# A fused transformer forward pass on one core: order of work in attention block one's last six steps, and the split of the convolution's last group between engines

## The chip, the core and the metric

The kernel runs on one core of a Trainium2 chip. The metric is the device time of one execution in microseconds (us). Before the change the median of three runs is 1892.98 us (1890.98 to 1897.77). Every time below is from one profiled execution of that kernel, which took 1893.7 us and whose first to last instruction span 1891.7 us; "at 237.29" means 237.29 us after the span's start.

## What is computed

Two transformer blocks run over 512 tokens of width 1024 (batch 1). The parts that matter here are the attention of block one and the convolution of block two's odd layer:

```python
# block one: differential attention, 8 heads of 2 x 64, in query blocks of 128
s1 = einsum('bhqd,bkhd->bhqk', qa, k1) + bias      # bias = -slope * |pq - pos|
s2 = einsum('bhqd,bkhd->bhqk', qb, k2) + bias
a = softmax(s1) - lam * softmax(s2)
o = einsum('bhqk,bkhd->bqhd', a, v)
o = rmsnorm(o, subln_g) * (1.0 - lam_init)         # over a head's 128
x = x + g1 * (o.reshape(B, S, H * dv) @ w_out)
# block two, odd layer: gated projection, depthwise convolution of 31 taps, layer norm, projection
h = h[..., :CONV_DIM] * sigmoid(h[..., CONV_DIM:])
y = causal_dwconv(h, dw_w, dw_b)                   # width 31, 1024 channels
y = silu(layer_norm(y, ln_g, ln_b)) @ w_pw2
```

Between and after them stand a mixture of 16 experts, a second attention with pooling, and two gated feed-forward layers with a convolution of width 3.

## The kernel before

Everything is kept transposed, channels on the 128 partitions and the 512 tokens along the row; `x` is eight such chunks (KC = 8). Each weight chunk of 128 x 1024 floats is split by ScalarE into a rounded part (`split_hi`, line 118) and by VectorE into the rest (`split_lo`, line 123), and `product` (lines 950 to 960) multiplies with three matmuls: high by high, low activation by high weight, low weight by high activation. The order on each engine is written by hand; the engines meet through semaphores, and each engine's queue is strictly in order. PSUM is the one tensor `ps`, 8 banks of 128 x 512 floats.

**Attention of block one.** A step g (0 to 31) is one head (g // 4) and one query block of 128 (g % 4). On TensorE a step has `scores` (line 1019, two 128 x 512 results, into banks 0 and 1 for even g, 2 and 3 for odd g), `turn` (line 1029, four transposes of the combined probabilities into bank 4) and `values` (line 1040, four matmuls). VectorE has `biased` (line 1652, adds the distance bias and takes the row maximum; line 1658 negates it), `combined` (lines 1666, 1668 and 1671, softmax one minus lambda times softmax two), and `copy_o` (line 1677). ScalarE has `exps` (line 567, two halves), `evict_turned` (line 575) and `squares_of_o` (line 583). While the loop runs over g, TensorE makes scores two steps ahead; VectorE does `combined(g + 1)`, then `biased(g + 2)`, then `copy_o(g)`. In steps 0 to 25 TensorE fills the rest of each step with half a projection of queries or keys (`qk_part`). From step CARRY = 26 on there is no such projection left; TensorE turns a finished head's output back (`turn_o(g - 26)`, line 1051), ScalarE and VectorE make its two parts (`o_hi`, line 593; `o_lo`, line 1692). After the loop come `turn_o(5)` and `turn_o(6)`, then the output projection: `two_products` makes output chunks 0 and 1 together, input chunk by input chunk (k = 0 to 7, six matmuls each, with `turn_o(7)` ahead of k = 4), and the chunks m = 2 to 7 follow one at a time in banks 4 and 5, each after `x_new` of chunk m - 2. VectorE adds each to `x` (line 1737) and in between works through columns of the conditioning matrix (`late_column`, line 1602).

**Convolution.** Channel chunks are called groups q = 0 to 7. Of a group's 31 taps, ScalarE with GpSimd makes 9 (products at line 894, sums at line 2292), TensorE 6 (`taps`, line 1524, a matmul with a diagonal matrix that ScalarE has built, line 885) and VectorE 16 (`taps_dve`, lines 2142 and 2148), accumulating in PSUM; lines 2152 and 2154 add the parts. Group 7 stands behind the loop. Then the layer norm: TensorE sums the channels with a matmul by ones (`rms_sum`, line 923), VectorE scales the mean (line 1563), TensorE spreads it over partitions (`spread`, line 929), VectorE subtracts it from all eight chunks (line 2180), ScalarE squares them (line 477), and TensorE sums the squares, this time after `wait_ge(centred, KC)`, all eight subtractions. `unread` (line 935) issues matmuls whose results nobody reads: one ahead of chunk 7's sum, two behind it, four behind the spread, in both passes.

## Time and profile before

| | |
|---|---|
| median of 3 runs | 1892.98 us |
| the profiled execution, and its span | 1893.7 us, 1891.7 us |
| TensorE matmuls busy | 1815.9 us |
| VectorE, ScalarE, GpSimd busy | 1188.0, 907.8, 184.3 us |
| mean granted TensorE clock | 0.972 |
| attention's last steps and first two output chunks | about 225 to 266 us |
| the convolution's group 7 and its layer norm | about 1425 to 1467 us |

### The profile page before, as it was taken

Reading aid. Unit: us, or ns where it says so; the run is one execution under the profiler, and the core shown is the slowest. Engines: PE = TensorE matmul, PEld = TensorE weight load, DVE = VectorE, ACT = ScalarE, POOL = GpSimd, SP = SyncE. Lnnn points to the kernel's source line nnn. Section 1 sums busy time; section 2 is a strip of 40 time slices with the busy share of each in tenths; the row PEclk is TensorE's granted clock in tenths of the full one; section 3 lists DMA queues with packets and bytes.
Section 4 is the critical chain, followed back from the end, with each engine's and each line's share of the span. In section 5 each row is a group of like instructions: output and inputs, shape, how many; then the busy total and the mean of one; then the engine's idle time right before and its main releaser. Section 6 shows DMA issues by size and latency. Waiting matters only on the chain.

```text
span 1891.7 us, 26051 instructions
## 1 busy us (share of the span) xinstructions
PE 1815.9 (96%) x8494; PEld 1408.8 (74%) x8494; DVE 1188.0 (63%) x1838; ACT 907.8 (48%) x1379; POOL 184.3 (10%) x219
## 2 busy tenths in 40 slices
PE   7999989899999789999999999999996999999999
PEld 5777677688888567667788888886663778888887
DVE  6777775788898572454566665224997566656422
ACT  3566641488788534554444434115663544444310
POOL 0000000222322100001000000001763000000000
PEclk8999988699999989999999999999997999999999
DMA  9533141899999451111233233331210222332331
GB/s 401 178 101 98 48 135 66 316 347 374 381 376 367 172 182 49 45 41 34 78 102 98 89 103 109 99 89 45 67 67 23 78 78 89 100 100 89 112 99 56
DMA packets 72785, 259.20 MB, mean 137 GB/s; under 512 B 10256, under 2 KB 10384, under 8 KB 71440
## 3 DMA queue, kind: packets, MB, share of 16 engines
q1 hardware_dynamic: 67536, 247.85, 37.7%
q0 software_dynamic: 4608, 8.40, 1.2%
q10 hardware_dynamic: 576, 2.10, 0.3%
q8 instruction: 40, 0.66, 0.1%
q14 instruction: 25, 0.20, 0.0%
HBM read 254.11 MB, written 12.58 MB: 141 GB/s over the span
## 4 chain that ended last, share of the span: by engine, by line
PE 89%; DVE 4%; issue 2%; ACT 2%; DMA 1%; SPq 0%; DVEq 0%; POOL 0%; ACTq 0%; POOLq 0%
PE ps L958 19%; PE ps L960 19%; PE ps L959 19%; PE ps L1140 3%; PE ps L1141 3%; PE ps L1142 3%; PE ps L935 2%; PE ps L1524 2%; PE ps L1160 1%; PE ps L1162 1%; PE ps L1161 1%; PE ps L1019 1%; PE ps L1040 1%; PE ps L978 1%; PE ps L979 1%
## 5 line engine op out<-in xcount | busy, mean ns | idle before, releaser
L958 PE MATMUL ps<-h_hi,w_hi 128*128 128x512 f32 x1184 | 473.9, 400 | 0.7 <-DVE x L1737 0.5
L960 PE MATMUL ps<-h_hi,w_lo 128*128 128x512 f32 x1184 | 462.3, 390 | 0.0
L959 PE MATMUL ps<-h_lo,w_hi 128*128 128x512 f32 x1184 | 461.7, 390 | 0.0
L123 DVE TENSOR_TENSOR w_lo<-raw,w_hi 128x1024 fp32r<-128x1024 f32 x212 | 266.4, 1260 | 190.1 <-ACT w_hi L118 184.9
L118 ACT ACTIVATE w_hi<-raw 128x1024 fp32r<-128x1024 f32 x212 | 221.5, 1049 | 205.4 <-PE ps L960 168.6
L958 PEld LDWEIGHTS ps<-h_hi,w_hi 128*128 128x128 f32 x1184 | 222.7, 188 | 75.6 <-issue 31.8
L960 PEld LDWEIGHTS ps<-h_hi,w_lo 128*128 128x128 f32 x1184 | 222.6, 188 | 47.4
L959 PEld LDWEIGHTS ps<-h_lo,w_hi 128*128 128x128 f32 x1184 | 222.9, 188 | 46.9 <-issue 2.9
L2091 DVE SCALAR_TENSOR_TENSOR tmp<-ps,param,tmp 128x511 f32<-128x511 f32 (+1 forms) x176 | 131.8, 749 | 133.4 <-ACT tmp L846 121.4
L162 DVE TENSOR_TENSOR w_lo<-ring,w_hi 128x1024 fp32r<-128x1024 f32 x128 | 149.9, 1220 | 30.6 <-ACT w_hi L158 30.5
L846 ACT ACTIVATE tmp<-ps,param 128x512 f32<-128x512 f32 x88 | 68.5, 779 | 179.5 <-PE ps L960 179.5
L958 PE MATMUL ps<-gv_hi,w_hi 128*128 (+1 forms) x352 | 139.1, 395 | 0.0
L960 PE MATMUL ps<-gv_hi,w_lo 128*128 (+1 forms) x352 | 139.0, 395 | 0.0
L959 PE MATMUL ps<-gv_lo,w_hi 128*128 (+1 forms) x352 | 139.0, 395 | 0.0
L158 ACT ACTIVATE w_hi<-ring 128x1024 fp32r<-128x1024 f32 x128 | 128.7, 1055 | 12.3 <-PE ps L1142 12.3
L2202 POOL TENSOR_TENSOR pool_carrier<-const 128x1 f32<-128x1 f32 x74 | 33.9, 459 | 678.1 <-DVE x L2115 432.8
L2292 POOL TENSOR_TENSOR part<-prod,part 128x512 f32<-128x512 f32 x64 | 84.8, 1326 | 55.4 <-ACT prod L894 51.0
L1140 PE MATMUL ps<-w_hi,e_hi 128*128 128x512 f32 x192 | 78.9, 411 | 5.6 <-DVE e_lo L1828 5.6
L960 PEld LDWEIGHTS ps<-gv_hi,w_lo 128*128 128x128 f32 x352 | 66.0, 187 | 16.2
L162 DVE TENSOR_TENSOR m_lo<-ring,m_hi 128x1024 fp32r<-128x1024 f32 x64 | 76.6, 1219 | 2.3 <-ACT m_hi L158 2.3
L959 PEld LDWEIGHTS ps<-gv_lo,w_hi 128*128 128x128 f32 x352 | 66.0, 187 | 16.2
L958 PEld LDWEIGHTS ps<-gv_hi,w_hi 128*128 128x128 f32 x352 | 66.0, 187 | 16.1
(310 smaller groups left out, 2782.1 us busy)
## 6 DMA issues: line engine op xcount, KB each, us to landing
ring<-in_w_m SPq DMA_DIRECT2D x192, 512.0 KB, 5.8
raw<-in_w_b SPq DMA_DIRECT2D x180, 512.0 KB, 3.5
raw<-in_w_a SPq DMA_DIRECT2D x32, 512.0 KB, 4.0
ada_late<-in_ada_b SPq DMA_DIRECT2D x32, 512.0 KB, 4.4
ada<-in_ada_a SPq DMA_DIRECT2D x8, 1024.0 KB, 17.0
y_tok<-y_dram SPq DMA_DIRECT2D x8, 512.0 KB, 6.9
x<-in_x SPq DMA_DIRECT2D x2, 1024.0 KB
h_dram<-h_tok ACTq DMA_DIRECT2D x4, 512.0 KB, 3.5
```

The costliest lines, as they stand in the source:

```text
L118: act.activation(self.hi[:, s, :], self.raw[:, s, :], ACT.Copy).then_inc(self.hi_done, 1)
L123: dve.tensor_tensor(self.lo[:, s, :], self.raw[:, s, :], self.hi[:, s, :].bitcast(F32), ALU.subtract).then_inc(self.lo_done, 1)
L158: act.activation(self.hi[c % PARTS_M], self.ring[:, c % RING], ACT.Copy).then_inc(self.hi_done, 1)
L162: dve.tensor_tensor(self.lo[c % PARTS_M], self.ring[:, c % RING], self.hi[c % PARTS_M].bitcast(F32), ALU.subtract).then_inc(self.lo_done, 1)
L846: act.activation(tmp[:, c], ps[:, c], ACT.Identity, scale=PR_at("ffn_w", it, 6, 3 * p + (f * 2 + val) * 3 * FC + 2), bias=PR_at("ffn_b", i ...
L958: pe.matmul(dst, hi, a_hi, start=first, stop=False, skip_group_check=True)
L959: pe.matmul(dst, hi, a_lo, start=False, stop=False, skip_group_check=True)
L960: return pe.matmul(dst, lo, a_hi, start=False, stop=last, skip_group_check=True)
L1140: pe.matmul(ps[:, bank], e_hi[:, k], hi, start=(k == 0), stop=False, skip_group_check=True)
L1141: pe.matmul(ps[:, bank], e_lo[:, k], hi, start=False, stop=False, skip_group_check=True)
L2091: dve.scalar_tensor_tensor(out=tmp[:, c, back:], in0=ps[:, c, 0:T - back], scalar=PR_at("ffn_w", it, 6, 3 * p + (f * 2 + val) * 3 * FC + tap),
L2292: pool.tensor_tensor(part[:, p], prod[:, n % 4], part[:, p], ALU.add).then_inc(part_step, 1)
```

## The change

It has two parts. **In attention**, from step 26 on, all scores go to banks 0 and 1 (`s_bank`) and each waits for `biased` of the step before; TensorE makes scores three steps ahead instead of two (in step 26 both `scores(28)` and `scores(29)`); VectorE does `biased(g + 2)` ahead of `combined(g + 1)`; banks 2 and 3, now free, hold output chunks 0 and 1, whose share of input chunk k is issued by `first_outputs(k)`, k = 0 to 3 inside steps 28 to 31, k = 4 behind `turn_o(6)`, then `turn_o(7)` (now in bank 7) and k = 5 to 7. Output chunks 2 and 3 no longer wait for an addition to `x`; chunk m from 4 on waits for chunk m - 2 as before.

**In the convolution**, group 7 gets 16 taps on TensorE and 6 on VectorE (`last_taps`). The ten additional diagonal matrices lie in the first half of `act_out` and are made by ScalarE ahead of the convolution's loop. VectorE accumulates its six taps in banks 6 and 0, adds them up, adds GpSimd's part, and last TensorE's. In the mean's pass the `unread` matmuls ahead of and behind chunk 7's sum are gone (the four behind the spread stay), and TensorE no longer waits for all eight subtractions ahead of the sums of squares; each sum waits for its own square.

TensorE, last steps of attention. Here `hd_qk` rows are `scores`, `const,tmp` rows `turn`, `v,at_pt` rows `values`, `const,o` rows `turn_o`, and `h_hi,w_hi` to `h_hi,w_lo` a `product`. Before, from `scores(28)` on:

```order
L1019 MATMUL ps<-hd_qk 128x512 x2
L1029 MATMUL ps<-const,tmp 128x128 x4
L1040 MATMUL ps<-v,at_pt 128x128 x4
L1051 MATMUL ps<-const,o 128x128 x4
L1019 MATMUL ps<-hd_qk 128x512 x2
L1029 MATMUL ps<-const,tmp 128x128 x4
L1040 MATMUL ps<-v,at_pt 128x128 x4
L1051 MATMUL ps<-const,o 128x128 x4
L1019 MATMUL ps<-hd_qk 128x512 x2
```

After, from `scores(28)` on:

```order
L1031 MATMUL ps<-hd_qk 128x512 x2
L1041 MATMUL ps<-const,tmp 128x128 x4
L1052 MATMUL ps<-v,at_pt 128x128 x4
L1063 MATMUL ps<-const,o 128x128 x4
L1031 MATMUL ps<-hd_qk 128x512 x4
L1041 MATMUL ps<-const,tmp 128x128 x4
L1052 MATMUL ps<-v,at_pt 128x128 x4
L1063 MATMUL ps<-const,o 128x128 x4
L1031 MATMUL ps<-hd_qk 128x512 x2
L1041 MATMUL ps<-const,tmp 128x128 x4
L1052 MATMUL ps<-v,at_pt 128x128 x4
L1063 MATMUL ps<-const,o 128x128 x4
```

`scores(29)` and `scores(30)` now stand together behind `turn_o(0)`, the latter a step earlier than before; behind the last row shown come six matmuls of `first_outputs(0)`.

VectorE in step 26. `hd_bias` rows are `biased`, the rows with `at_r`, `at_c` and `tmp<-tmp,at_c` are `combined`, `o<-o,o_r` is `scale_o(4)` and `o<-ps,at_r` is `copy_o(26)`. Before:

```order
L1666 RECIPROCAL at_r<-at_sum 128x2
L1668 TENSOR_SCALAR at_c<-at_r,at_sum,neg_lam 128x1
L1671 SCALAR_TENSOR_TENSOR tmp<-tmp,at_c 128x512
L1650 MEMSET carrier 128x1
L1652 ISA tmp,at_m<-ps,hd_bias 128x512
L1652 ISA at_m 128x1
L1652 ISA tmp,at_m<-ps,hd_bias 128x512
L1652 ISA at_m 128x1
L1658 TENSOR_SCALAR at_nm<-at_m 128x2
L1688 TENSOR_TENSOR o<-o,o_r 128x4x128
L1677 TENSOR_SCALAR o<-ps,at_r 128x128
```

After:

```order
L1681 MEMSET carrier 128x1
L1683 ISA tmp,at_m<-ps,hd_bias 128x512
L1683 ISA at_m 128x1
L1683 ISA tmp,at_m<-ps,hd_bias 128x512
L1683 ISA at_m 128x1
L1689 TENSOR_SCALAR at_nm<-at_m 128x2
L1697 RECIPROCAL at_r<-at_sum 128x2
L1699 TENSOR_SCALAR at_c<-at_r,at_sum,neg_lam 128x1
L1702 SCALAR_TENSOR_TENSOR tmp<-tmp,at_c 128x512
L1719 TENSOR_TENSOR o<-o,o_r 128x4x128
L1708 TENSOR_SCALAR o<-ps,at_r 128x128
```

`biased(28)` moved ahead of `combined(27)`, and so in each of steps 26 to 29.

TensorE behind the convolution's loop, before (`glu,diag` is `taps`, `conv,ones` and `tmp,ones` are the sums, `ps<-const` is `unread`, `junk,const` is `spread`):

```order
L1524 MATMUL ps<-glu,diag 128x512 x6
L923 MATMUL ps<-conv,ones 32x128 x28
L935 MATMUL ps<-const 128x512
L923 MATMUL ps<-conv,ones 32x128 x4
L935 MATMUL ps<-const 128x512 x2
L929 MATMUL ps<-junk,const 128x128 x4
L935 MATMUL ps<-const 128x512 x4
L923 MATMUL ps<-tmp,ones 32x128 x28
```

After:

```order
L1556 MATMUL ps<-glu,diag 128x512 x6
L1556 MATMUL ps<-glu,act_out 128x512 x10
L934 MATMUL ps<-conv,ones 32x128 x32
L940 MATMUL ps<-junk,const 128x128 x4
L946 MATMUL ps<-const 128x512 x4
L934 MATMUL ps<-tmp,ones 32x128 x28
```

Ten matmuls with a diagonal came in ahead of the sums, and three `unread` matmuls went.

The diff, without the declarations of banks and semaphores that the words above give:

```diff
         def o_bank(h):
-            return SSQ if h < 5 else h - 5
+            return SSQ if h < 5 or h == H - 1 else h - 5
+        def s_bank(g):
+            return 0 if g >= CARRY else g % 2 * 2
+        def p_bank(m):
+            return 2 + m if m < 2 else 4 + m % 2
...
         STEPS = NT * H
...
+            for j in range(LAST_MORE):
+                act.activation(diag_last[:, j], C("ident"), ACT.Copy,
+                               scale=PR("dw_w", (KC - 1) * TAPS + POOL_TAPS + PE_TAPS + j, 1)).then_inc(diag_more, 1)
             conv_act(0, True)
...
                 conv_act(it, False)
...
                 for k in range(first, KC):
-                    if k == KC - 1:
+                    if k == KC - 1 and n != MEAN:
                         unread(1)
                     rms_sum(n, k, src)
-                unread(2)
+                if n != MEAN:
+                    unread(2)
                 pe.wait_ge(rstd_done, n + 1)
...
                 unread(4)
...
                 if g >= 2:
-                    pe.wait_ge(s_free, g - 1)
+                    pe.wait_ge(s_free, g if g > CARRY else g - 1)
                 for half in range(2):
                     d = slice(half * DH, (half + 1) * DH)
-                    last = pe.matmul(ps[:, g % 2 * 2 + half], hd_qk[d, h % 2, 0, q * P:(q + 1) * P], hd_qk[d, h % 2, 1, :],
+                    last = pe.matmul(ps[:, s_bank(g) + half], hd_qk[d, h % 2, 0, q * P:(q + 1) * P], hd_qk[d, h % 2, 1, :],
                                      start=True, stop=True, skip_group_check=True)
...
                     pe.wait_ge(acc_free, 2 * H)
-                elif h < 5:
-                    pe.wait_ge(hlo_done, KC + h)
+                elif h < 5 or h == H - 1:
+                    pe.wait_ge(hlo_done, KC + min(h, 5))
                 pe.wait_ge(o_scaled, h + 1)
...
                 last.then_inc(o_tr, 1)
+            def first_outputs(k):
+                parts_made(k, KC)
+                for m in range(2):
+                    if k == 0:
+                        sa.ready(pe, 6, m)
+                    last = product(ps[:, p_bank(m)], sa.parts(m, k), k, k == 0, k == KC - 1)
+                    if k == KC - 1:
+                        last.then_inc(sa.used, 1)
...
             for half in range(2):
...
             for g in range(STEPS):
-                if g + 2 < STEPS:
+                if g <= CARRY:
                     scores(g + 2)
+                elif g + 3 < STEPS:
+                    scores(g + 3)
                 if g < CARRY:
...
                 if g + 1 < STEPS:
...
                     turn_o(g - CARRY)
-            def last_heads(k):
-                if k == 4:
-                    turn_o(H - 1)
+                if g == CARRY:
+                    scores(g + 3)
+                if g >= CARRY + 2:
+                    first_outputs(g - CARRY - 2)
...
             turn_o(H - 2)
+            first_outputs(4)
+            turn_o(H - 1)
+            for k in range(5, KC):
+                first_outputs(k)
             pe.wait_ge(o_copied, STEPS - 1)
-            two_products(6, 0, 4, lambda k: KC, sa, last_heads)
             for m in range(2, KC):
                 sa.ready(pe, 6, m)
-                pe.wait_ge(x_new, m - 1)
+                if m >= 4:
+                    pe.wait_ge(x_new, m - 1)
                 for k in range(KC):
-                    last = product(ps[:, 4 + m % 2], sa.parts(m, k), k, k == 0, k == KC - 1)
+                    last = product(ps[:, p_bank(m)], sa.parts(m, k), k, k == 0, k == KC - 1)
                 last.then_inc(sa.used, 1)
...
                 pe.wait_ge(sq_done, q + (MEAN * KC - 1))
-                for j in range(PE_TAPS):
-                    last = pe.matmul(ps[:, 4 + p], diag[:, p, j], glu[:, p, POOL_TAPS + j:POOL_TAPS + j + T],
-                                     start=(j == 0), stop=(j == PE_TAPS - 1), skip_group_check=True)
+                more = LAST_MORE if isinstance(q, int) and q == KC - 1 else 0
+                if more:
+                    pe.wait_ge(diag_more, more)
+                for j in range(PE_TAPS + more):
+                    by = diag[:, p, j] if j < PE_TAPS else diag_last[:, j - PE_TAPS]
+                    last = pe.matmul(ps[:, 4 + p], by, glu[:, p, POOL_TAPS + j:POOL_TAPS + j + T],
+                                     start=(j == 0), stop=(j == PE_TAPS + more - 1), skip_group_check=True)
                 last.then_inc(pe_taps, 1)
             def chunk_pair(it, first):
...
             rms_sums(MEAN, src=conv, first=KC - 2)
-            pe.wait_ge(centred, KC)
             rms_sums(7)
...
             ffn_pe(1, 8, 6 * KC + NG, 28, 2)
...
                     last = dve.tensor_tensor_reduce(
-                        out=at_p[:, g % 2 * 2 + half], in0=ps[:, g % 2 * 2 + half],
+                        out=at_p[:, g % 2 * 2 + half], in0=ps[:, s_bank(g) + half],
                         in1=hd_bias[:, h % 2, (NT - 1 - q) * P:(NT - 1 - q) * P + T], scale=1.0, scalar=-BIG,
...
                 last.then_inc(s_free, 1)
...
             for g in range(STEPS):
+                if g >= CARRY and g + 2 < STEPS:
+                    biased(g + 2)
                 if g + 1 < STEPS:
...
                     o_lo(g - CARRY - 1)
-                if g + 2 < STEPS:
+                if g < CARRY:
                     biased(g + 2)
...
                     sa.split_lo(dve, 0, KC + 3 + g // 2 + AHEAD)
...
                 sa.multiplied(dve, 6, m)
-                dve.scalar_tensor_tensor(out=x[:, m], in0=ps[:, 4 + m % 2], scalar=mod[:, 2 * KC + m:2 * KC + m + 1],
+                dve.scalar_tensor_tensor(out=x[:, m], in0=ps[:, p_bank(m)], scalar=mod[:, 2 * KC + m:2 * KC + m + 1],
                                          in1=x[:, m], op0=ALU.mult, op1=ALU.add).then_inc(x_new, 1)
...
+            def last_taps():
+                q, p, own, fresh = KC - 1, 1, ps[:, 5], (ps[:, RB], ps[:, 0])
+                count = DVE_TAPS - LAST_MORE
+                for n in range(count):
+                    j = TAPS - count + n
+                    src, w, acc = glu[:, p, j:j + T], PR("dw_w", q * TAPS + j, 1), fresh[n % 2]
+                    if n >= 2:
+                        dve.wait_ge(dve_tap, q * DVE_TAPS + (n - 1))
+                        ins = dve.scalar_tensor_tensor(out=conv[:, q] if n == count - 2 else acc, in0=src, scalar=w, in1=acc,
+                                                       op0=ALU.mult, op1=ALU.add)
+                    elif n:
+                        ins = dve.tensor_scalar(acc, src, w, None, ALU.mult)
+                    else:
+                        ins = dve.tensor_scalar(acc, src, w, PR("dw_b", q, 1), ALU.mult, ALU.add)
+                    ins.then_inc(dve_tap, 1)
+                dve.wait_ge(dve_tap, q * DVE_TAPS + count)
+                dve.tensor_tensor(conv[:, q], conv[:, q], fresh[1], ALU.add).then_inc(dve_tap, 1)
+                dve.wait_ge(part_done, q + 3)
+                dve.wait_ge(dve_tap, q * DVE_TAPS + count + 1)
+                dve.tensor_tensor(conv[:, q], conv[:, q], part[:, p], ALU.add).then_inc(merged, 1)
+                dve.wait_ge(pe_taps, q + 3)
+                dve.wait_ge(merged, q + 1)
+                dve.tensor_tensor(conv[:, q], conv[:, q], own, ALU.add).then_inc(sq_done, 1)
             def conv_pair(it, first):
                 for c in range(SLOTS):
...
                 conv_pair(it, False)
-            taps_dve(KC // 2 - 1, 1)
+            last_taps()
             rms_spread(MEAN, mean=True)
...
             for k in range(KC):
```

## Rows read from the trace of the kernel before

**Rows 1.** Page, part 1: busy time, share of the span, instructions.

```profile
PE 1815.9 (96%) x8494; PEld 1408.8 (74%) x8494; DVE 1188.0 (63%) x1838; ACT 907.8 (48%) x1379; POOL 184.3 (10%) x219
```

**Rows 2.** Timeline, TensorE, 226 to 255: start, us, engine, line, names, [idle before <- releaser].

```profile
226.94 0.66 PE L1029 MATMUL ps<-const,tmp 128*128 128x128 f32 x4 [0.75 <-DVE tmp L1671]
...
228.85 1.13 PE L1019 MATMUL ps<-hd_qk 64*128 64x512 f32 x4
...
237.29 0.66 PE L1029 MATMUL ps<-const,tmp 128*128 128x128 f32 x4 [2.57 <-DVE tmp L1671]
237.78 1.06 PE L1040 MATMUL ps<-v,at_pt 128*128 128x128 f32 x8
...
248.46 1.11 PE L1029 MATMUL ps<-const,tmp 128*128 128x128 f32 x4 [2.73 <-DVE tmp L1671]
```

**Rows 3.** Timelines of VectorE and ScalarE, one step of attention (237.99 to 243.38).

```profile
237.99 0.69 DVE L1652 CUSTOM_DVE_ANT_0 tmp<-ps,hd_bias 128x512 f32<-128x512 f32 x1
...
241.08 0.17 DVE L1666 RECIPROCAL at_r<-at_sum 128x2 f32<-128x2 f32 x1 [1.33 <-ACT tmp L567]
...
243.38 0.75 DVE L1692 SCALAR_TENSOR_TENSOR h_lo<-ps,subln,h_hi 128x512 fp32r<-128x512 f32 x1 [1.03 <-ACT h_hi L593]
...
239.53 0.72 ACT L567 ACTIVATE tmp<-tmp,at_nm 128x512 f32<-128x512 f32 x1 [2.25 <-DVE at_nm L1658]
```

**Rows 4.** Timelines around the output projection's third chunk: TensorE, then VectorE.

```profile
266.45 0.47 PE L958 MATMUL ps<-h_hi,w_hi 128*128 128x512 f32 x1 [0.47 <-DVE x L1737]
...
272.08 0.43 PE L923 MATMUL ps<-tmp,ones 128*32 128x128 f32 x8
...
274.64 0.74 DVE L1737 SCALAR_TENSOR_TENSOR x<-ps,mod,x 128x512 f32<-128x512 f32 x1
```

**Rows 5.** Windows of 1 us: busy time of each engine, granted clock (PEclk), DMA.

```profile
1427.00:1428.00 1.00, 1.00 (x3) 0.48 (x2) 1.00 (x2) 1.00 (x3) 0.12 (x1) 0.82 0.89 295
...
1431.00:1432.00 1.00, 1.00 (x4) 0.52 (x3) 1.00 (x2) 0.37 (x2) 0.92 (x2) 0.97 0.00 0
```

**Rows 6.** Timeline, VectorE, the convolution's group 7 and the mean.

```profile
1437.53 0.81 DVE L2142 TENSOR_SCALAR ps<-glu,param 128x512 f32<-128x512 f32 x1
1438.24 8.64 DVE L2148 SCALAR_TENSOR_TENSOR ps<-glu,param,ps 128x512 f32<-128x512 f32 x13
...
1448.31 0.70 DVE L2152 TENSOR_TENSOR ps<-ps,part 128x512 f32<-128x512 f32 x1
1449.04 0.69 DVE L2154 TENSOR_TENSOR conv<-conv,ps 128x512 f32<-128x512 f32 x1
1450.50 0.29 DVE L1563 TENSOR_SCALAR junk<-ps 128x128 f32<-128x128 f32 x1 [0.78 <-PE ps L923]
1455.52 4.87 DVE L2180 TENSOR_TENSOR conv<-conv,ps 128x512 f32<-128x512 f32 x8 [4.72 <-PE ps L929]
```

**Rows 7.** Timeline, TensorE, the same stretch.

```profile
1426.68 7.08 PE L1524 MATMUL ps<-glu,diag 128*128 128x512 f32 x12 [2.56 <-issue]
1433.69 1.52 PE L923 MATMUL ps<-conv,ones 128*32 128x128 f32 x48
...
1449.78 0.65 PE L923 MATMUL ps<-conv,ones 128*32 128x128 f32 x8 [9.61 <-DVE conv L2154]
1450.37 3.78 PE L935 MATMUL ps<-const 128*128 128x512 f32 x4
1453.94 1.54 PE L929 MATMUL ps<-junk,const 128*128 128x128 f32 x8
...
1466.31 1.05 PE L929 MATMUL ps<-junk,const 128*128 128x128 f32 x8
```

**Rows 8.** Timeline, ScalarE: group 0's diagonals, the next sigmoid, squares and root of the norm.

```profile
1312.06 1.85 ACT L885 ACTIVATE diag<-const,param 128x128 f32<-128x128 f32 x6
...
1327.63 0.60 ACT L882 ACTIVATE sig<-ps 128x512 f32<-128x512 f32 x1 [4.33 <-PE ps L960]
...
1464.63 0.37 ACT L504 ACTIVATE junk<-ps,const 128x128 f32<-128x128 f32 x1 [1.44 <-PE ps L923]
```

4 lines of the change are left out of this document (3 added, 1 removed).

## Prediction

> **What bounds the kernel now.** I read the page first: TensorE is busy 1815.9 of 1891.7 us [rows 1], so only stretches where it idles or works for nobody can give anything. The timelines show two of these, and they are where the change is. In attention's last steps TensorE stands 0.75 to 2.73 us ahead of each transpose, released by VectorE's last operation on the probabilities [rows 2]. Behind the convolution's loop it stands 9.61 us, released by VectorE's line 2154, the last addition of group 7 [rows 7]; VectorE is continuously busy there [rows 6]. Past both stretches everything waits for TensorE or moves with it, so what they lose the whole span loses. The profiled execution took 1893.7 us, 0.7 above the median; I sum against 1893.7 and leave that 0.7 in.
>
> **Attention, the cycle before.** The chain of one step is a ring. `biased` starts at 237.99, ScalarE's first exponential at 239.53 (1.54 later), `combined` at 241.08 (1.55 later), and `o_lo` at 243.38 after 1.03 of waiting, so `combined` ended at 242.35 (1.27 after its start) [rows 3]. `biased` of the next step stands behind that `o_lo` (0.67 from start to start). So 1.54 + 1.55 + 1.27 + 1.03 + 0.67 = 6.1 in an even step; an odd step has no wait for `o_hi` and is shorter. The transposes of steps 27, 29 and 31 start at 226.94, 237.29 and 248.46 [rows 2]: 5.4 a step on average.
>
> **Attention, the new cycle.** `biased(g + 2)` now stands ahead of `combined(g + 1)`, so ScalarE's 3.1 for the exponentials lie beside VectorE's `combined`, `o_lo` and copy. Moved with it is a wait: `combined(27)` is queued behind `biased(28)`, which needs `scores(28)`, and all of step 26 on TensorE is queued behind `turn(27)`. I walked the three queues from step 26 with the durations of rows 2 and 3 and of the rows around them; the same walk of the old order gives 231.35, 237.36, 242.59 and 248.60 for the transposes of steps 28 to 31, within 0.15 of the trace. The new order gives:
> - `scores(28)` ends at 226.94 - 0.75 = 226.19, as now [rows 2]; `biased(28)` from 226.25, `combined(27)` from 227.64, so `turn(27)` at 228.96, **2.0 later** than now, after a pause of 2.83.
> - `scores(29)` can only follow `turn_o(0)`: 230.88, and takes 1.13 as at 228.85 [rows 2]. `biased(29)` 232.07, `scores(30)` 233.43 (one pair of banks, so each waits for the `biased` before), `turn(28)` 234.78.
> - Then VectorE is the bound with some 4.6 a step: `turn(29)` 239.43, `turn(30)` 243.96, `turn(31)` 247.35. That is only 1.1 ahead of 248.46 [rows 2]; the transition ate the rest.
> - From there TensorE is the bound. Before, it went from 248.46 to 266.45, where output chunk 2 starts after 0.47 of waiting for `x` [rows 4]: 18.0. Now it has: transposes 0.47, values 0.92, a pause of 0.62, `turn_o` 0.53, and the values of step 31 at 0.92 (0.49 from the start of a transposition to the values at 237.78 [rows 2]); three more `turn_o`, 1.59; and six of the eight `first_outputs`, k = 2 to 7. One is six matmuls; 24 went from 266.45 to 272.08 [rows 4], with the last one's start 0.235 each, so 1.43 with its edges, 8.6 in all. Sum 13.6, chunk 2 at 260.98. `first_outputs(0)` and `(1)`, 2.9, lie in pauses where VectorE is the bound and cost nothing; if those pauses are gone they cost 2.9.
>
> So at full clock the stretch gives 266.45 - 260.98 = **5.5**. What is late next: chunk 4 waits for `x` of chunk 2. Its addition starts at 274.64 [rows 4] behind columns that VectorE works through alone, once it has the last head's `o_lo`; by the walk that comes 3.7 earlier, so the addition ends at 274.64 + 0.7 - 3.7 = 271.6, and TensorE comes to chunk 4 at 260.98 + 2 x 6.0 = 273.0. It stays hidden, by 1.4. The columns' loads are paced by VectorE as before.
>
> **The clock takes part of it back.** A pause of 2.56 at 1424.1 made the granted clock fall: 0.82 in the window from 1427, back to 0.97 in that from 1431 [rows 5], a low stretch of some 3.3. The transposes at 248.46 took 1.11 against 0.66 [rows 2], after pauses of 2.57 and 2.29. The new pause of 2.83 is longer than any of these. If the clock falls some 0.7 behind its end, the remaining 2.3 of work up to `scores(29)`, all on the chain, take twice as long: +2.2. I take this, since the pauses at full clock were mostly followed by a fall. **Attention: -3.3**, ends -5.5 (no fall) and +4.9 (low until the first output chunks).
>
> **Convolution, VectorE's side.** Group 7 starts at 1437.53 and its sum is ready at 1449.04 + 0.69 = 1449.73 [rows 6]. Thirteen taps took 8.64 with 0.75 for the last, so they stand (8.64 - 0.75) / 12 = 0.66 apart [rows 6]. Ten fewer: -6.6. One more addition of the dependent kind, 1449.04 - 1448.31 = 0.73 [rows 6]: +0.7. VectorE would have the sum at 1443.9.
>
> **TensorE's side.** The six taps of group 7 ran from 1426.68 to 1433.69, 7.0 for 12 instructions [rows 7]. This holds the low stretch of some 3.3, worth 1.8; at full clock a tap is (7.0 - 1.8) / 6 = 0.86. Sixteen: 13.8 + 1.8 = 15.6, to 1442.3. Behind them are queued the sums of chunks 0 to 6, at 1.52 for six [rows 7], 1.8: 1444.1. These were hidden in VectorE's time; now TensorE comes to chunk 7's sum at 1444.1 and VectorE at 1443.9. The two meet, and the later one counts: the sum of chunk 7 starts at 1444.1 instead of 1449.78.
>
> **The mean's pass.** Today VectorE has the scaled mean at 1450.50 + 0.29 = 1450.79, but the spread starts only at 1453.94, since two `unread` matmuls take 1450.37 to 1453.94 at the low clock [rows 7]. They go: -3.1. With TensorE busy up to 1444.1 I take the full clock, where the spread is 1.05 (1466.31) and not 1.54 [rows 7]. So 1444.1, +0.50 to VectorE, +0.29, +0.06, +1.1: the subtractions start at 1446.1 instead of 1455.52 [rows 6], **-9.4**.
>
> **The squares' pass.** The wait for all eight subtractions (4.87 [rows 6]) goes. ScalarE needs sums of squares 0 to 3 read before it can reuse its four buffers; they now follow the four `unread` behind the spread, at 1446.1 + 3.35 = 1449.45, and not the last subtraction. ScalarE goes on at 1449.8 and the root follows 3.6 later as now: 1453.4 against 1464.63 [rows 8]. That is 7.3 after the subtractions' start instead of 9.1: -1.8. **Convolution: -11.2.**
>
> **ScalarE's ten diagonals.** Six took 1.85 [rows 8], ten take 2.9. They stand ahead of group 0's sigmoid, which may come up to 2.9 later. VectorE then has nothing to do before the second sigmoid at 1327.63, for which ScalarE waited 4.33 [rows 8]. Cost 0; were that cover gone, up to 2.9.
>
> A rule of the Trainium skill speaks against taking `unread` out: "TensorE: Matmul & The Clock Gate", section "Why this matters for your kernels", advises against pauses between bursts of matmuls, since they lower the clock. The trace agrees for today's pause of 9.61, behind which `unread` takes 0.9 an instruction [rows 7]. What it would do where the pause is small is the third rival.
>
> **Sum.** 1893.7 - 3.3 - 11.2 = **1879.2**.
>
> **Rivals.**
> - *The clock doesn't fall in step 26.* For it: one pause of 2.57 at full clock, at 237.29 [rows 2], saw no fall at once. 1893.7 - 5.5 - 11.2 = 1877.0.
> - *Attention gives nothing*: the low stretch reaches into the steps bounded by VectorE, or the covered 2.9 of `first_outputs` comes out. For it: today's low stretch there lasts long enough to show in the transposes at 248.46. Then 1893.7 - 11.2 = 1882.5. The wait that was removed has been replaced by the 2.83.
> - *The norm runs at the low clock.* Then the spread is 0.5 longer, the sum 0.2, and the four `unread` take 6.9 instead of 3.4, all ahead of the first sum of squares: 4.2 less of gain, 1883.4. Against it: TensorE idles little from 1426.7 on.
> - *Slower than before: the clock stays low through both places.* Attention at +4.9; the sixteen taps at 1.72 take 27.5, to 1454.2, the seven sums 3.5, the subtractions start at 1460.4, +4.9, less 1.8 to 2.0 for the squares: 1893.7 + 4.9 + 2.9 = 1901.5. TensorE's side costs more than VectorE's gives back from about 22 us of low clock within the taps. Against it: dense work brought the clock back after 3.3 [rows 5].
> - *The change doesn't do what it says*, that is, the taps' split is right but the removed wait gains nothing: 1.8 less, 1881.0, inside the range.
>
> **How the numbers follow.** Chances: forecast 0.47, clock holds 0.25, attention nothing 0.12, norm low 0.08, slower 0.03, the rest (something behind the two stretches takes back a few us) 0.05. The range 1875.5 to 1884.5 takes in the first four. The measurement can tell about 0.5% (9.5 us) from no change, so faster means under 1883.5: the first three, half of the fourth, some of the rest, 0.90. Within 0.5%: 0.07. Slower: 0.03.
>
> **What would show it.** TensorE's wait ahead of the transpose of step 27 about 2.8, later ones under 1.5; scores three steps ahead; output chunk 2 starting 3 to 6 us earlier; the clock in the window behind step 26's pause; sixteen taps ending near 1442.3 less attention's gain; the last addition and chunk 7's sum within 0.5 of each other; 1.3 to 1.7 from that sum's start to the spread's end; the root some 7.3 behind the first subtraction. Wrong would be: a pause ahead of `scores` (the one pair of banks), VectorE waiting more than 1 us for the taps, or output chunk 4 waiting for `x`.

## The result, and the profile after

The changed kernel has a median of 1876.51 us (1874.39 to 1878.32, 4 runs) against 1892.27 us of the kernel before (4 runs) beside it: ratio 0.9911, 95% interval 0.9897 to 0.9924. Measured again beside the last experiments it came to 1878.67 us (1874.16 to 1880.91, 6 runs) against 1893.72 (11 runs): 0.9919, 0.9904 to 0.9933. Over all ten runs its median is 1877.62 us. The forecast was 1879.2. The profiled execution of the result took 1874.39 us (span 1872.6), outside the range given, and that is a separate question: of its 19.3 us against the profiled execution of before, 3.8 are not in the code that changed.

The page of the kernel after, part 1 (busy time, share, instructions), against [rows 1]:

```profile
PE 1811.0 (97%) x8508; PEld 1404.5 (75%) x8508; DVE 1181.4 (63%) x1829; ACT 911.4 (49%) x1389; POOL 186.3 (10%) x219
```

TensorE has fourteen instructions more (twenty for ten taps, six fewer of `unread`), and its busy time still fell by 4.9, since less of it ran at the low clock (mean granted clock 0.984 against 0.972). The rest of the gain is idle time that went.

**Attention.** Timeline of TensorE, kernel after, steps 26 to 31 (start, duration, engine, line, names; in brackets the idle time before and who ended it). The rows to lay beside it are [rows 2]:

```profile
228.94 0.66 PE L1041 MATMUL ps<-const,tmp 128*128 128x128 f32 x4 [2.92 <-DVE tmp L1702]
229.43 1.06 PE L1052 MATMUL ps<-v,at_pt 128*128 128x128 f32 x8
230.33 0.60 PE L1063 MATMUL ps<-const,o 128*128 128x128 f32 x4
230.86 1.13 PE L1031 MATMUL ps<-hd_qk 64*128 64x512 f32 x4
233.53 1.13 PE L1031 MATMUL ps<-hd_qk 64*128 64x512 f32 x4 [1.54 <-DVE at_m L1683]
234.90 0.66 PE L1041 MATMUL ps<-const,tmp 128*128 128x128 f32 x4 [0.25 <-DVE tmp L1702]
...
239.56 0.66 PE L1041 MATMUL ps<-const,tmp 128*128 128x128 f32 x4 [0.24 <-DVE tmp L1702]
...
244.16 0.66 PE L1041 MATMUL ps<-const,tmp 128*128 128x128 f32 x4 [1.24 <-DVE tmp L1702]
...
247.58 0.66 PE L1041 MATMUL ps<-const,tmp 128*128 128x128 f32 x4
...
266.12 0.43 PE L934 MATMUL ps<-tmp,ones 128*32 128x128 f32 x8
```

The transposes were predicted for 228.96, 234.78, 239.43, 243.96 and 247.35. The durations of 0.66 say that the clock stayed full. Output chunk 2 starts at 260.59, predicted for 260.98. The last row is the sum behind output chunk 2, at 272.08 before [rows 4]: 5.96 earlier. No row of TensorE between 258 and 276 shows a wait, so chunk 4 does not wait for `x`.

**Convolution, group 7 and the mean.** Timelines of TensorE, VectorE and ScalarE, kernel after, against [rows 6, 7, 8]:

```profile
1416.96 5.39 PE L1556 MATMUL ps<-glu,diag 128*128 128x512 f32 x12 [2.56 <-issue]
1422.18 8.75 PE L1556 MATMUL ps<-glu,act_out 128*128 128x512 f32 x20
1430.86 1.74 PE L934 MATMUL ps<-conv,ones 128*32 128x128 f32 x56
1434.25 0.42 PE L934 MATMUL ps<-conv,ones 128*32 128x128 f32 x8 [1.65 <-DVE conv L2212]
1435.09 1.21 PE L940 MATMUL ps<-junk,const 128*128 128x128 f32 x8 [0.41 <-DVE junk L1594]
1436.09 5.29 PE L946 MATMUL ps<-const 128*128 128x512 f32 x8
1441.31 1.08 PE L934 MATMUL ps<-tmp,ones 128*32 128x128 f32 x32
...
1433.51 0.69 DVE L2212 TENSOR_TENSOR conv<-conv,ps 128x512 f32<-128x512 f32 x1
1434.74 0.29 DVE L1594 TENSOR_SCALAR junk<-ps 128x128 f32<-128x128 f32 x1 [0.55 <-PE ps L934]
1436.34 4.87 DVE L2238 TENSOR_TENSOR conv<-conv,ps 128x512 f32<-128x512 f32 x8 [1.30 <-PE ps L940]
...
1441.87 2.19 ACT L485 ACTIVATE tmp<-conv 128x512 f32<-128x512 f32 x4 [2.38 <-PE ps L934]
1445.49 0.37 ACT L512 ACTIVATE junk<-ps,const 128x128 f32<-128x128 f32 x1 [1.44 <-PE ps L934]
```

Counted from the first tap, which takes out all that happened earlier: the first subtraction was at 28.84 (1455.52 - 1426.68) and is at 19.38 (1436.34 - 1416.96), -9.46. The root was at 37.95 (1464.63 - 1426.68) and is at 28.53, -9.42. From the first subtraction to the root it was 9.11 and is 9.15: the squares' pass gained nothing. Windows of 1 us of the same kernel (busy time of each engine; the third number from the end is the granted clock) show what stood in the way:

```profile
1435.00:1436.00 1.00, 0.91 (x8) 0.91 (x9) 0.04 (x1) 0.00 (x0) 0.00 (x0) 1.00 0.00 0
1436.00:1437.00 1.00, 1.00 (x5) 0.48 (x4) 0.66 (x2) 0.00 (x0) 0.00 (x0) 0.54 0.00 0
1437.00:1438.00 1.00, 1.00 (x3) 0.48 (x2) 1.00 (x3) 0.94 (x2) 0.00 (x0) 0.50 0.00 0
1438.00:1439.00 1.00, 1.00 (x3) 0.48 (x2) 1.00 (x3) 1.00 (x3) 0.00 (x0) 0.50 0.00 0
1439.00:1440.00 1.00, 1.00 (x3) 0.26 (x2) 1.00 (x3) 0.48 (x1) 0.00 (x0) 0.76 0.00 0
```

TensorE waited 1.65 ahead of chunk 7's sum, and at 1436 the clock fell to 1.2 GHz. The four `unread` took 5.29 instead of some 3.6 and ended at 1441.31, just as the last subtraction did (1436.34 + 4.87 = 1441.21). So in this profile the four `unread` had taken the place of the removed wait: the sums of squares start no earlier than with it.

**The middle.** From the chunk sum to group 7's first tap the two kernels run the same code, apart from ScalarE's ten diagonals. It took 1154.60 before (272.08 to 1426.68) and 1150.84 after. From the root to the end the span has 427.07 and 427.11. The whole difference is then -5.96 - 3.76 - 9.42 + 0.04 = -19.1 of span, and 0.2 outside it. The 3.76 is not shown to be an effect of the change; the section on the prediction comes back to it.

### The profile page after: what moved, and what is told of

Read it like the earlier page. It is cut to its first block, busy times and chain, and to the rows that moved or that the text cites. A ratio compares the mean times of both kernels' runs of the same rounds, so it can differ in the third digit from the quotient of the medians.

```text
span 1872.6 us, 26081 instructions
## 1 busy us (share of the span) xinstructions
PE 1811.0 (97%) x8508; PEld 1404.5 (75%) x8508; DVE 1181.4 (63%) x1829; ACT 911.4 (49%) x1389; POOL 186.3 (10%) x219
## 4 chain that ended last, share of the span: by engine, by line
PE 85%; DVE 6%; issue 4%; ACT 2%; DMA 2%; DVEq 0%; SPq 0%; POOL 0%; ACTq 0%; POOLq 0%
PE ps L970 19%; PE ps L972 18%; PE ps L971 18%; PE ps L1168 3%; PE ps L1170 3%; PE ps L1169 3%; PE ps L946 2%; PE ps L1031 2%; PE ps L1188 1%; PE ps L1190 1%; PE ps L1189 1%; PE ps L1052 1%; DMA raw<-in_w_a 1%; PE ps L1380 1%; PE ps L934 1%
```

## The experiments

Each is the changed kernel with the edit shown, except for the second. Every ratio is to the kernel before on the same chip.

**The two parts, one at a time.** `attn_only` keeps attention's part and takes back the convolution's:

```diff
-LAST_MORE = 10
+LAST_MORE = 0
...
-                    if k == KC - 1 and n != MEAN:
+                    if k == KC - 1:
...
-                if n != MEAN:
-                    unread(2)
+                unread(2)
...
+            pe.wait_ge(centred, KC)
...
-            last_taps()
+            taps_dve(KC // 2 - 1, 1)
```

> The attention part alone; the convolution and its norm as before the change. Theory A (the parts add up, what lies elsewhere is the clock's chance): output chunk 2 of block one starts 5.5 us earlier than before where no low clock falls between 225 and 255, 2.5 to 3.5 where one falls behind the pause of 2.9 in step 26; median 3 to 7 us under before, about 1887.5. Theory B (the 4 us that the changed kernel gained between attention and the convolution are an effect of the attention part, such as weights that come earlier): 8 to 10 us under before, about 1883, with the shift against before growing behind 270 at the same places as in the changed kernel.

Measured: 1888.53 us against 1893.09, ratio 0.9976 (0.9966 to 0.9985). Ten runs from 1884.73 to 1891.73; the profiled one is the fastest, with 5.95 less up to the chunk sum, a middle of 1151.41, and the root 9.11 behind the first subtraction. By medians attention is worth 4.6, inside the 3 to 7 of theory A; theory B wanted 8 to 10.

`conv_only` is the kernel before with the convolution's and ScalarE's part of the diff.

> The convolution part alone; attention as before the change. Theory A: 9.4 to 11.2 us under before, about 1882; the subtractions of the mean start 9.4 earlier, and the root of the norm comes 7.3 behind them where the clock is full there, 9.1 where it falls behind the pause ahead of chunk 7's sum. Theory B (part of the convolution's gain needs the earlier attention): under 8 us, above 1885. A third view, that the fall of the clock at the spread is chance, expects both 7.3 and 9.1 to be seen among the runs of these kernels; if it follows from the new pauses, 9.1 in all.

Measured: 1883.29 us against 1893.09, ratio 0.9947 (0.9931 to 0.9964), so 9.8. Its middle is 1154.06, and the root is again 28.53 behind the first tap, with the 1.66 pause and the low clock behind it, as in the profile of after. From the first subtraction to the root it is 8.81 here (9.15 in after), so of the two values that the expectation allowed it is nearer to 9.1. The parts add: 4.6 + 9.8 = 14.4, where the two measurements of the whole change gave 15.8 and 15.1, and the prediction's terms add to 14.5.

**Step 26: what the new order costs to enter.** `old26` keeps `combined(27)` ahead of `biased(28)` in step 26 alone:

```diff
-                if g >= CARRY and g + 2 < STEPS:
+                if g > CARRY and g + 2 < STEPS:
...
-                if g < CARRY:
+                if g <= CARRY:
```

> The changed kernel, but in step 26 VectorE does combined(27) ahead of biased(28) as before the change; from step 27 on the new order. If the transition costs what the walk says, the pause ahead of turn(27) is 0.75 and not 2.92, turn(31) comes 2.0 earlier and output chunk 2 starts 2.0 earlier than in the changed kernel: about 1874.5. If steps 27 on are bound by a chain that does not pass through turn(27), such as scores and the one pair of banks, nothing changes: about 1876.5.

Measured: 1874.39 us (1871.14 to 1876.39), ratio 0.9896 (0.988 to 0.9913). The interval overlaps that of the changed kernel, so the median alone does not show the 2 us; the trace does. TensorE's timeline of `old26`:

```profile
226.99 0.66 PE L1041 MATMUL ps<-const,tmp 128*128 128x128 f32 x4 [0.75 <-DVE tmp L1702]
...
232.95 1.12 PE L1041 MATMUL ps<-const,tmp 128*128 128x128 f32 x4 [0.25 <-DVE tmp L1702]
233.86 1.92 PE L1052 MATMUL ps<-v,at_pt 128*128 128x128 f32 x8
```

The transpose of step 27 is back at 226.99, against 226.94 before the change [rows 2] and 228.94 with it: the transition cost 2.0 (2.2 by the pauses, 2.92 against 0.75). Here the clock fell anyway, a step later (1.12 and 1.92 instead of 0.66 and 1.06), behind a pause of 1.54 and one of 0.25. Even so the chunk sum is at 265.40. So the fall does not need the pause of 2.92.

**The covered part of the output projection.** `fo_behind` issues `first_outputs(0)` to `(3)` behind the loop:

```diff
-                if g >= CARRY + 2:
-                    first_outputs(g - CARRY - 2)
...
-            first_outputs(4)
+            for k in range(5):
+                first_outputs(k)
```

> The changed kernel with first_outputs(0) to (3) issued behind the loop, right ahead of first_outputs(4), instead of inside steps 28 to 31. If the first two lie in pauses and cost nothing where they are, as the walk has it, transposes of steps 28 to 31 start where they do in the changed kernel (234.90, 239.56, 244.16, 247.58) and the first sum of squares of block one comes 2.9 later, at about 269.0, with the clock at 1.00. If they delay steps 29 to 31 inside the loop, less than 2.9. The longer pauses may also let the clock fall, which would show in the transposes' durations and cost more.

Measured: 1881.65 us, ratio 0.9932 (0.9912 to 0.9952). TensorE's timeline of `fo_behind`:

```profile
244.14 0.66 PE L1041 MATMUL ps<-const,tmp 128*128 128x128 f32 x4 [2.61 <-DVE tmp L1701]
244.63 1.77 PE L1052 MATMUL ps<-v,at_pt 128*128 128x128 f32 x8
...
248.22 1.12 PE L1041 MATMUL ps<-const,tmp 128*128 128x128 f32 x4 [0.96 <-DVE tmp L1701]
```

With `first_outputs(0)` gone from ahead of it, the transpose of step 30 starts at 244.14 instead of 244.16, after 2.61 of idle time instead of 1.24: those six matmuls were free. In the changed kernel `first_outputs(1)` was covered too: `combined(31)` ends there at 247.52, and the transpose of step 31 starts at 247.58. The chunk sum of `fo_behind` comes at 270.35, 4.2 later. The estimate for the two that were covered was 2.9. The rest goes with the low clock that followed the 2.61 and lasted up to 251.7; the expected 269.0 was for the full clock.

**The four `unread` behind the mean's spread.** `no_four` takes them out of the mean's pass:

```diff
-                unread(4)
+                if n != MEAN:
+                    unread(4)
```

> The changed kernel without the four unread matmuls behind the mean's spread. Theory: these four, and not the wait that was removed, hold the sums of squares back; then the root comes 7.0 to 7.3 behind the first subtraction instead of 9.15, 2 us less, about 1874.5. Rival: they keep the clock up, and without them it falls behind the spread, so that the sums, the second spread and the first products run at half speed: 0 to 2 us more than the changed kernel, about 1877.5.

Measured: 1878.27 us, ratio 0.9924 (0.9907 to 0.994). TensorE and ScalarE behind the spread:

```profile
1439.97 1.72 PE L940 MATMUL ps<-junk,const 128*128 128x128 f32 x8 [0.41 <-DVE junk L1595]
1443.13 4.24 PE L934 MATMUL ps<-tmp,ones 128*32 128x128 f32 x56 [1.44 <-ACT tmp L485]
...
1448.85 0.37 ACT L512 ACTIVATE junk<-ps,const 128x128 f32<-128x128 f32 x1 [1.58 <-PE ps L934]
```

The root is 7.13 behind the first subtraction (at 1441.72) although the clock is low (4.24 for 56 small matmuls): at the low clock the four cost 2.0 in this pass. First tap to root is 27.02 against 28.53. The median shows none of these 1.5; in attention this kernel's profile had a fall that after's had not (transposes of 1.12 at 228.81, the chunk sum at 267.57 instead of 266.12). That accounts for the profile and not for the median: the expected 1874.5 was missed, and whether the 1.5 is there in most executions is not shown.

**One `unread` into the pause.** `one_back` gives the mean's pass back the one ahead of chunk 7's sum; `one_back_wait` also the removed wait:

```diff
-                    if k == KC - 1 and n != MEAN:
+                    if k == KC - 1:
```

```diff
+            pe.wait_ge(centred, KC)
```

> The changed kernel with one unread matmul of the mean's pass back: the one ahead of chunk 7's sum, where TensorE waits 1.65 us for VectorE in the changed kernel. Theory (the 1.8 of the squares' pass is missing because the clock falls behind that pause): the pause shrinks to some 0.8, the clock stays at 1.00 over the spread and the four unread, which then take 3.6 and not 5.3, and the root comes 7.2 behind the first subtraction instead of 9.15; median 1.5 to 2 us under the changed kernel, about 1874.8. Rival (the four unread take long for a reason of their own, or the clock falls all the same): 8.8 to 9.2 behind, same time as the changed kernel.

> As one_back, and TensorE again waits for all eight subtractions ahead of the sums of squares. If the removed wait is worth its 1.8 once the clock is full, the root comes 9.1 behind the first subtraction again, 1.8 later than in one_back. If ScalarE's squares are the bound in any case, both come equally late.

Measured: 1880.12 us, ratio 0.9921 (0.9903 to 0.9939), and 1880.42 us, 0.9918 (0.9896 to 0.9941). TensorE and ScalarE of `one_back`:

```profile
1425.42 7.09 PE L1556 MATMUL ps<-glu,diag 128*128 128x512 f32 x12 [2.56 <-issue]
...
1442.69 1.13 PE L946 MATMUL ps<-const 128*128 128x512 f32 x2
...
1445.58 3.60 PE L946 MATMUL ps<-const 128*128 128x512 f32 x8
1449.11 1.08 PE L934 MATMUL ps<-tmp,ones 128*32 128x128 f32 x32
...
1453.29 0.37 ACT L512 ACTIVATE junk<-ps,const 128x128 f32<-128x128 f32 x1 [1.44 <-PE ps L934]
```

and of `one_back_wait`:

```profile
1442.88 3.60 PE L946 MATMUL ps<-const 128*128 128x512 f32 x8
1448.01 1.08 PE L934 MATMUL ps<-tmp,ones 128*32 128x128 f32 x32 [1.53 <-DVE conv L2239]
```

Both kernels have the four at 3.60, full clock. Without the wait the root is 7.51 behind the first subtraction (1445.78); with it 9.11 (1443.08 to 1452.19), and TensorE idles 1.53 for the last subtraction. So the removed wait is worth 1.6 where the clock is full, and at most 0.3 where the four `unread` run slowly (9.15 in after, 8.94 in `old26`, 8.81 in `conv_only`). These profiles also had a low stretch within the taps (7.09 instead of 5.39), so they do not prove that the one `unread` kept the clock up. The median of `one_back` was expected at 1874.8 and is 1880.12; its ratio has an interval that overlaps the changed kernel's, so no gain is shown and no loss either.

**The three `unread`.** `unread_back` gives the mean's pass all three back, the wait stays removed:

```diff
-                    if k == KC - 1 and n != MEAN:
+                    if k == KC - 1:
...
-                if n != MEAN:
-                    unread(2)
+                unread(2)
```

> The changed kernel with the mean's pass as before the change: one matmul that nobody reads ahead of chunk 7's sum and two behind it. The removed wait stays removed. The prediction put the two behind the sum at 3.1 of low clock ahead of the spread; at the full clock they are 1.8. Theory: with the taps split 16 to 6 TensorE comes into the norm at the full clock, the two cost 1.0 to 1.8 ahead of the spread, and since the pause ahead is filled the root is 7.5 behind the first subtraction; from first tap to root 28.5 to 29.5 (28.53 in after), so the three cost 0 to 1 in all. Rival (they hold the spread up at the low clock as before the change): spread 3 us later than in after and first tap to root 31.5.

Measured: 1879.86 us, ratio 0.9925 (0.9909 to 0.9942). First tap to root 29.10 (1421.31 to 1450.41), root 7.51 behind the first subtraction, the two behind the sum 1.8 at full clock. Against 27.87 of `one_back` (1425.42 to 1453.29) these two cost 1.2. The next experiment has a profile without any of the three whose taps had the same low stretch, with 26.84: against that all three cost 2.3, and the one of `one_back` 1.0. The 0 to 1 of the expectation was counted from after's 28.53, a profile with another course of the clock.

**The changed kernel once more.**

> The changed kernel once more, to see how much of its profiled time is repeatable. Theory (parts add, and the stretch between attention and the convolution, whose code is the same in both kernels, is 1150.8 to 1156.6 us long by where the low clock falls): median 1874 to 1879, the taps of group 7 start 1153.5 to 1156.6 behind the first chunk sum in most executions and not 1150.8 as in the profile of after; the norm's root 28.5 behind the first tap, 9.1 behind the first subtraction. Rival (the change itself shortens the middle stretch by 3.8): again 1150.8 there, and a median at or under 1875.

Measured as given above; the profiled execution took 1874.94. It differs from the first profile in where the clock was low. TensorE, VectorE and ScalarE:

```profile
1419.17 7.09 PE L1556 MATMUL ps<-glu,diag 128*128 128x512 f32 x12 [2.56 <-issue]
...
1434.77 2.12 PE L934 MATMUL ps<-conv,ones 128*32 128x128 f32 x64
...
1438.30 3.60 PE L946 MATMUL ps<-const 128*128 128x512 f32 x8
...
1435.72 0.69 DVE L2212 TENSOR_TENSOR conv<-conv,ps 128x512 f32<-128x512 f32 x1
1438.50 4.87 DVE L2238 TENSOR_TENSOR conv<-conv,ps 128x512 f32<-128x512 f32 x8 [1.25 <-PE ps L940]
...
1446.01 0.37 ACT L512 ACTIVATE junk<-ps,const 128x128 f32<-128x128 f32 x1 [1.44 <-PE ps L934]
```

The expectation of 28.5 from first tap to root was wrong: it is 26.84, and 7.51 behind the first subtraction. The low stretch fell into the taps. That costs TensorE 1.70, but VectorE's last addition ends 17.24 behind the first tap in both profiles (1433.51 + 0.69 - 1416.96; 1435.72 + 0.69 - 1419.17), so all of the 1.70 is hidden. TensorE then does all 64 instructions of the sums in one go, there is no pause ahead of chunk 7's, and the norm runs at full clock. The stage is 1.7 faster with a low stretch in the taps than without. Other profiles say the same of the kernels that have ten taps more on TensorE and none of the three `unread`:

| profile | taps of 12 instructions | wait ahead of chunk 7's sum | clock over spread and four `unread` | first tap to root |
|---|---|---|---|---|
| after, `conv_only`, `old26` | 5.39 | 1.65 to 1.66 | falls | 28.53, 28.53, 28.54 |
| `after_again`, `fo_behind` | 7.09 | none | full | 26.84, 26.84 |

`no_four`, with 5.39 and 1.66, had the fall too. The wait and the absence of an earlier low stretch always come together here, so which of them brings the fall is not shown; a profile with the pause filled and full clock in the taps would tell, and there is none. The median went against the rival; the middle of 1151.35 went for it.

**A version that does better.** `more11_old26` has `old26`'s edit and one tap more on TensorE (11 more, 5 left on VectorE, whose adding up then reads the other of its two banks); `old26_one_back` has `old26`'s and `one_back`'s.

> Two edits on the changed kernel: step 26 in the old order, as in old26, and 11 more taps on TensorE instead of 10 (5 on VectorE). TensorE waits 1.65 for VectorE ahead of chunk 7's sum in the changed kernel; with one tap more it comes 0.86 later and VectorE 0.66 earlier, so they meet. Expected: chunk 7's sum 0.6 to 0.66 earlier, the pause 0.1 to 0.3, the clock full over the spread, the root 7.2 behind the first subtraction: 2.4 in the norm and 0.7 to 2.0 in attention, about 1873. Rival: no gain in the norm, since the sums themselves let the clock fall; then 1874 to 1875 like old26.

> The changed kernel with two edits: in step 26 VectorE keeps combined(27) ahead of biased(28), and one matmul that nobody reads is back ahead of chunk 7's sum in the mean's pass. Theory (the two places are independent): transpose of step 27 at 226.8 with 0.75 of idle time as before the change, first chunk sum at 263.8 at the full clock or 265.4 if the clock falls in those steps (266.1 in the profile of after); in the norm no low clock behind chunk 7's sum and the root 7.5 behind the first subtraction, not 9.1; median 1 to 3 us under after_again. Rival (the gain of either place is lost again to low clock somewhere else, as with the single matmul alone, which came out at 1880): the places measure as said, but the median is at or above that of after_again.

Measured: 1875.76 us, ratio 0.9901 (0.9883 to 0.992), and 1873.27 us (1871.73 to 1877.21), ratio 0.9888 (0.9873 to 0.9903). `more11_old26` had full clock in attention, with the transposes of steps 27 and 28 at 226.61 and 232.58 and the chunk sum at 263.81, 2.3 ahead of after's. In its taps, which the clock slowed as well, VectorE had to wait:

```profile
1435.00 0.69 DVE L2212 TENSOR_TENSOR conv<-conv,ps 128x512 f32<-128x512 f32 x1 [0.78 <-PE ps L1556]
```

so ten is the better number there: first tap to root is 27.54 against the 26.84 of ten. How eleven does with full clock in the taps was not seen. In attention, the chunk sum of `more11_old26` comes 37.20 behind the transpose of step 27, that of after 37.18, so only the way up to that transpose differs. `old26_one_back` was 5.4 faster than the changed kernel beside it, and the intervals of the two ratios just miss each other. Part of that can be the clock, which each result gives as a mean over the execution, and comparing at equal mean clock does not settle how much:

| mean clock | changed kernel | `old26` | `old26_one_back` |
|---|---|---|---|
| 0.984 | 1874.16, 1874.39 | 1871.14 | 1871.73, 1872.34 |
| 0.983 | 1874.94, 1875.31 | 1874.37, 1874.41 | 1874.20 |
| 0.977 to 0.979 | 1879.79, 1880.47, 1880.91 | 1876.39 | 1877.21 |

The difference is 1.8 to 3.3 us in the first row, 0.5 to 1.1 in the second and 2.6 to 4.5 in the third. All twelve runs of the three kernels with `old26`'s edit have a median of 1874.39, the ten of the changed kernel 1877.62, on different chips. So a gain from the old order in step 26 is likely, of the size of the 2.0 in the trace, and the rest of the 5.4 is open. The one `unread` shows no gain of its own: `old26` alone, with 1874.39, is not told apart from 1873.27.

## Why the prediction came out as it did, point by point

The profiled execution took 4.8 less than the forecast and lies below the range. The step that failed is the first paragraph's "Past both stretches everything waits for TensorE or moves with it": it puts everything outside the two places at nothing, and the only allowance for it was a chance of 0.05 that a few us would be taken back there. The profile showed 3.8 of gain in the unchanged middle instead. Without it this execution had come to 1878.2, inside the range, and the median of the four runs, 1876.51, is inside it in any case. In the changed places two errors partly cancel, which is luck: attention gave 5.96 and not 3.3, since the fall of the clock in step 26, priced at 2.2, did not come in this execution; the convolution gave 9.42 and not 11.2, since a fall that was not expected came in the norm. Together they gave 15.4 against the 14.5 forecast.

- **VectorE's and TensorE's sides of group 7 were right.** The sum was to be ready 17.2 behind the first tap (1443.9 - 1426.68): 17.24. TensorE was to come with its seven sums at 17.4, a low stretch in the taps included: in `after_again`, which had one, at 17.3 (1434.77 + 1.74 - 1419.17, with the 1.74 that 56 instructions took in after). In the profiled execution of the result the low stretch did not come, and the term of 1.8 was not there: TensorE had its seven sums at 15.6 (1430.86 + 1.74 - 1416.96). The same pause of 2.56 stands ahead of the first tap in all thirteen profiles; a low stretch in the taps followed in eight (7.08 or 7.09) and none in five (5.39). "A pause of 2.56 made the granted clock fall" was read from one of them.
- **The mean's pass was right**: -9.4 predicted, -9.46 and -9.51 (19.33 in `after_again`). Its split into terms was not: the two `unread` behind the sum were put at 3.1, which was their price in the old schedule at the low clock. In the new schedule they cost 1.2 and the one ahead of the sum 1.0, while the split of the taps with all three left in gives 7.2 (21.59 in `unread_back` against 28.84).
- **The squares' pass failed in the profiled execution.** The step at fault is "with TensorE busy up to 1444.1 I take the full clock". It was not busy: the taps ran at the full clock, so TensorE was 1.65 early and waited, and that short pause was followed by the fall. This is the third rival, the norm at the low clock, in part: it had been priced at 4.2 of less gain; it cost 1.6, since the spread was only 0.16 longer and the low stretch ended within the four `unread`. Where the taps had the low stretch that the prediction put there, the term came out: 7.51 against 7.3, and the stage -11.1 (37.95 to 26.84) against -11.2.
- **The cycle in attention was right.** Five transposes within 0.25 us, the price of the transition 2.0 (`old26`), the cover of `first_outputs(0)` (`fo_behind`), chunk 4's slack. The full-clock gain was put at 5.5 and is 5.96, of which 0.17 was there ahead of step 26.
- **The clock in step 26 is a term of its own, mis-sized and not settled.** Eight profiles have the new order in step 26: four had the fall behind its pause (`after_again`, `no_four`, `one_back`, `one_back_wait`), four did not (`after`, `attn_only`, `unread_back`, and `fo_behind`, which had one later). I priced it at 2.2 by doubling 2.3 of work. From the transpose of step 27 to the chunk sum after took 37.18, the three with one low stretch 38.54 to 38.82: it costs 1.4 to 1.6, because `scores(29)` at the end of that work already ran at the full clock again (1.13). It costs 2.6 in `one_back` (39.81), where the low stretch lasted twice as long. Windows of `after_again`, against 1.00 throughout in `after`:

```profile
228.00:229.00 1.00, 0.00 (x1) 0.01 (x1) 0.96 (x3) 1.00 (x3) 0.00 (x0) 1.00 0.00 0
229.00:230.00 1.00, 1.00 (x5) 1.00 (x6) 0.55 (x1) 1.00 (x3) 0.00 (x0) 0.51 0.00 0
...
232.00:233.00 1.00, 1.00 (x6) 0.57 (x6) 0.21 (x1) 0.74 (x3) 0.00 (x0) 0.78 0.00 0
```

- **ScalarE's ten diagonals cost nothing**, as predicted: group 1's sigmoid still waited, 3.76 instead of 4.33 [rows 8].
- **What the prediction didn't have is the middle: this is the step that put the execution outside the range.** It took the rest of the execution as fixed. Over thirteen profiles of twelve versions the same code between chunk sum and first tap took 1150.84 to 1156.64. Windows of 100 us from 300, for the kernel before, after, and `one_back`, in this order:

```profile
300.00:400.00 100.00, 89.12 (x433) 75.18 (x432) 71.06 (x123) 46.38 (x52) 15.03 (x25) 0.78 0.66 236
```

```profile
300.00:400.00 100.00, 88.73 (x431) 75.99 (x430) 77.21 (x128) 50.55 (x56) 18.25 (x31) 0.81 0.73 266
```

```profile
300.00:400.00 100.00, 89.11 (x413) 76.01 (x412) 71.94 (x123) 47.55 (x53) 14.98 (x25) 0.76 0.67 241
```

The granted clock there is 0.78, 0.81 and 0.76, and the middle 1154.60, 1150.84 and 1156.64. Summed over windows of 20 us from the chunk sum to the first tap, the low clock, worked out from each window's granted clock, lasts 65.2 us before, 58.0 in each of the three shortest middles (after, `after_again`, `attn_only`) and 68.4 in `one_back`. At half speed 7.2 us less of it are worth up to 3.6, by estimate nearly all of the 3.76. The sum alone does not fix the length, though: `conv_only` and `more11_old26` have 61.6 and 62.0, with middles of 1154.06 and 1154.62. The whole time varies within one kernel too: ten executions of the changed one took 1874.16 us (mean clock 0.984) to 1880.91 (0.979), with 1879.79 at 0.977. The range reached down to 1875.5 from the sum of the changed places alone; a range for one execution needs this spread of some 3 us to either side on top.

**What stays open.** The three short middles belong to the two profiles of the changed kernel and `attn_only`, all with the new order in step 26; but `no_four`, `one_back`, `one_back_wait`, `fo_behind` and `unread_back` have it too, with 1154.3 to 1156.6. Whether the change makes a favourable course of the clock likelier can't be told from one profile of each. Nor is it known why `one_back`, whose norm is shorter than after's by 0.7 in the profiles, has a slower median (1880.12 against 1877.62 over after's ten runs), unless by such chance. And what makes the clock fall behind one pause and not behind an equal one is not shown by any run here.

## What to carry to other kernels

Two engines that share a reduction should be balanced with the clock in mind: here VectorE sets the pace, so the low stretch in TensorE's taps is free, while the low stretch that followed a pause of 1.65 us just ahead of a serial chain cost 1.7. When a software pipeline is deepened in its last iterations, count the step in which the order switches: keeping the old order for that one step gave the transpose behind it back 2 us, of a part worth 4.6. And before a profiled difference is split into causes, measure how long the unchanged code between the changed places took in each profile.

## What the runs showed of the hardware that I had not expected

- A pause of 1.65 us of TensorE (`after`), and waits of 1.54 and 0.25 us with small matmuls between them (`old26`), were followed by a fall to 1.2 GHz; the 2.92 of `after` was not, and the same 2.92 in `after_again` was. The Trainium skill, "TensorE: Matmul & The Clock Gate", section "Why this matters for your kernels", warns of idle gaps between bursts of matmuls that are longer than these. The traces agree that a fall can follow a gap, but here it came behind shorter ones than the page warns of, and one and the same gap had two outcomes.
- Matmuls that nobody reads are not free. The four behind the spread took 5.29 us where the clock had fallen, and were then what the sums of squares waited for; without them the same pass, still at the low clock, was 2.0 shorter (`no_four`).
- A stage can be faster in an execution that has a low stretch in it: in the taps it cost nothing, and the norm behind it then ran at full clock, 1.7 us less from first tap to root (26.84 in two profiles against 28.53 and 28.54 in three).
